# Expert outputs scattered in pair order, x blocks turned by VectorE, gates applied in the final sum

## The chip, the cores and the metric

The kernel runs on one core of a Trainium2 chip. The metric is the device time of one execution in microseconds (us), the median of several runs. The program is written by hand for five engines: TensorE (PE in the profile, with its weight loads as PEld), VectorE (DVE), ScalarE (ACT), GpSimd (POOL) and SyncE (SP). They run their own instruction lists and meet at semaphores. Transfers are carried out by 16 DMA engines. SyncE issues plain transfers on the hardware queue q1. GpSimd issues indirect ones, with a row number per partition, on the software queue q0.

## The reference

The program computes one layer of a hybrid trunk for 128 context tokens and 512 latent tokens of width 1024 (float32): four groups of sequence mixers (gated DeltaNet, HGRN2, mLSTM, Hyena), an output projection, and then a mixture of experts with a final norm. The change concerns the mixture of experts:

```python
scores = sigmoid(t @ router_w)                    # t: 640 tokens x 1024, 64 experts
_, idx = top_k(scores + router_bias, 8)
sel    = take_along_axis(scores, idx)
wts    = sel / sum(sel) * 2.5                     # eight gates of a token
gates  = einsum('tk,tke->te', wts, one_hot(idx, 64))
hid    = silu(t @ w_gate[e]) * (t @ w_up[e])      # 1024 -> 128, every expert
routed = einsum('tef,efd->td', hid * gates[..., None], w_down)
x      = x + gate2 * (routed + shared)            # then the final RMSNorm
```

Only the eight chosen experts of a token have a gate that isn't zero, so a kernel may compute the 640 x 8 = 5120 pairs of token and expert alone.

## The kernel before

Everything up to the router takes until about 880 us and is not touched, but for one thing: between the chunks of the sequence mixers SyncE also fills the last 42 blocks of the DRAM tensor `y_rows` with zeros (L653), and waits for these fills at the end of that part.

**Slots.** The pairs are sorted by expert into blocks of 128 slots. Blocks 0 to 63 belong to the 64 experts, one each; an expert with more than 128 pairs has the rest in spill blocks from 64 on. Their number is known only at run time, in groups of two (`group_count`, at least `LEAST` = 2 groups beyond what is fixed). In these runs there are 70 blocks in all. VectorE makes one-hot matrices of the block and of the slot of every pair (L3070, L3072), ScalarE scales the block matrix by token number less 640 (L3275), and TensorE sums their products in `table(t)`, t = 0 to 4 (L2717). The result, plus 640, is `token_row`: the token of each slot, and 640 in an empty slot. A row number out of bounds is skipped by the indirect DMA. TensorE does these tables between the turning back of the normed x into rows, which SyncE stores to `h2_rows` with a token's 64 gates behind its 1024 values, and the products of the shared expert (L2728).

**A block.** The order on each engine is written out by hand, in a loop of 16 turns of `U` = 4 blocks:
- SyncE loads gate, up and down weights of block b, three transfers of 512 KB, into one of four buffers, once TensorE has done the down product of block b-4 (`load_block`, L2426 to L2428), and stores all 128 rows of an earlier y (`store_block`, L2432).
- GpSimd copies a column of `token_row` (L3400) and gathers 128 rows of x with its gates, 4352 bytes each, into one of four buffers (L3403), once the block four earlier has been turned.
- TensorE turns x by eight 128x128 transposes into PSUM (L2763), does the down product of the block before (L2779, 4 instructions of 512 columns in the trace) and then gate and up of this block (L2771, 32 instructions of 128 columns).
- ScalarE copies the turned x out of PSUM (L3310) and applies silu to the gate product (L3316).
- VectorE picks the gate column (L3089), multiplies silu(gate) by up (L3091), and evicts the down product with the gate as a scale (L3098).

Spill blocks (`spill`) go by pairs in buffers 0 and 1, with the expert read from `block_expert`. The load for such a block waits for the down product of the last block in the same buffer.

**Final sum.** When all stores have landed, GpSimd gathers for each tile of 128 tokens its eight y rows, choice by choice, by `dest_u` (40 indirect transfers of 512 KB, L3432) into `GB` = 14 buffers. TensorE sums choices 4 to 7 with the identity as the weights (L2820), VectorE sums choices 0 to 3 (L3151, L3157), adds the two (L3162), multiplies by gate2 (L3165) and adds to x (L3167). ScalarE sums the squares (L3336) and takes the root (L3339), VectorE scales (L3141), and SyncE stores the tile (L2472).

## Time and profile before

| | |
|---|---|
| runs | 1449.32 us median of 3 (1447.54 to 1451.58) |
| profiled execution | span 1449.8 us, 21596 instructions; no other time is recorded for it |
| busy PE, DVE, ACT, POOL | 1337.0, 685.5, 412.0, 301.5 us |
| TensorE clock | mean granted 0.983 |
| gate and up of block 0 starts | 922.87 us |
| down of the last block (69) starts | 1367.35 us |
| first read of the final sum | 1374.44 us |

The busy share of an engine says how full it is over the whole program, which has stages with different limits. So the shares are read by stage (a table of windows, times from the span's start), and then the chain of waits: the work that ended last, followed back from what each step waited for. The time of a transfer is counted as a share of the 16 DMA engines.

### The profile page before, as it was taken

What the parts mean: (1) busy time and instruction counts of PE and PEld (TensorE: products, weight loads), DVE (VectorE), ACT (ScalarE), POOL (GpSimd) and SP (SyncE); (2) the same over time, 40 slices, a digit from 0 to 9 for tenths busy, and PEclk for the clock granted to TensorE, in tenths of its full rate; (3) what the DMA queues carried; (4) which work ended last, traced back from release to release, by engine and by line L of the source; (5) the groups of instructions that cost most, each with busy time, mean ns of one, the idle gap of its engine ahead of it and who ended that gap; (6) DMA issues with size and microseconds to landing.
All of it is one profiled execution on the core that took longest, in us unless ns stands there. A gap on an engine that the chain in (4) does not pass through costs nothing. (4 is left out here: it accounts for less than half of the span.)

```text
span 1449.8 us, 21596 instructions
## 1 busy us (share of the span) xinstructions
PE 1337.0 (92%) x8160; PEld 996.5 (69%) x8160; DVE 685.5 (47%) x1254; ACT 412.0 (28%) x796; POOL 301.5 (21%) x440
## 2 busy tenths in 40 slices
PE   5999999999899998999799999999999999999664
PEld 1678666777899986555545457688888888887521
DVE  2698738202665663777576226432222222222156
ACT  3212221215556554233131025321222122212111
POOL 0200100102321311454440210211111111111173
PEclk9999999999999999999899999999999999999998
DMA  9656667121433341000120401799999999998696
GB/s 360 209 174 186 201 43 59 58 73 30 182 153 100 127 175 34 8 5 31 37 103 23 175 0 44 281 385 393 384 378 384 378 397 382 398 385 307 212 382 264
DMA packets 111005, 286.36 MB, mean 198 GB/s; under 512 B 28677, under 2 KB 46639, under 8 KB 109528
## 3 DMA queue, kind: packets, MB, share of 16 engines
q1 hardware_dynamic: 95096, 242.15, 48.6%
q0 software_dynamic: 15840, 43.28, 7.8%
q8 instruction: 45, 0.74, 0.2%
q14 instruction: 24, 0.20, 0.0%
HBM read 237.52 MB, written 64.56 MB: 208 GB/s over the span
## 5 line engine op out<-in xcount | busy, mean ns | idle before, releaser
L2771 PEld LDWEIGHTS PS<-arena 128*128 128x128 f32 x2240 | 258.5, 192 | 43.3 <-ACT arena L3310 26.2
L2771 PE MATMUL PS<-arena 128*128 128x128 f32 x2240 | 263.1, 276 | 5.2 <-DMA arena<-in_exp_w_down 3.9
L3098 DVE TENSOR_SCALAR arena<-PS,arena 128x1024 f32<-128x1024 f32 x70 | 89.9, 1284 | 141.6 <-PE PS L2779 141.6
L2779 PE MATMUL PS<-arena 128*128 128x512 f32 x280 | 137.8, 615 | 0.8 <-DVE arena L3091 0.8
L895 PE MATMUL PS<-arena 128*128 128x320 f32 x384 | 109.4, 438 | 1.5 <-DVE arena L1317 1.5
L3316 ACT ACTIVATE arena<-PS 128x128 f32<-128x128 f32 x70 | 19.4, 277 | 312.7 <-issue 176.7
L900 PE MATMUL PS<-arena 128*128 128x320 f32 x384 | 107.3, 432 | 0.0
L3091 DVE TENSOR_TENSOR arena<-arena,PS 128x128 f32<-128x128 f32 x70 | 20.1, 288 | 182.8 <-ACT arena L3316 93.4
L895 PEld LDWEIGHTS PS<-arena 128*128 128x128 f32 x384 | 73.0, 192 | 33.3 <-issue 2.9
L900 PEld LDWEIGHTS PS<-arena 128*128 128x128 f32 x384 | 73.0, 190 | 30.4
L3403 POOL DMA_INDIRECT arena<-h_rows,arena x70 | 72.1, 1030 | 58.4 <-POOL arena L3400 57.6
L3310 ACT ACTIVATE arena<-PS 128x1024 f32<-128x1024 f32 x70 | 71.6, 1023 | 43.6 <-PE PS L2763 43.6
L3400 POOL COPY arena<-arena 128x1 uint32 (+1 forms) x70 | 12.9, 185 | 309.5 <-DVE arena L3089 292.7
L1389 DVE SCALAR_TENSOR_TENSOR arena<-arena 128x1024 f32<-128x1024 f32 x56 | 69.1, 1280 | 15.5 <-DMA arena<-in_w_mod 14.9
L2763 PE MATMUL PS<-cst,arena 128*128 128x128 f32 x560 | 73.0, 273 | 1.6 <-DMA arena<-h_rows,arena 1.6
L2779 PEld LDWEIGHTS PS<-arena 128*128 128x128 f32 x280 | 47.4, 189 | 37.3 <-issue 34.5
L907 PE MATMUL PS<-arena 128*128 128x256 f32 (+1 forms) x320 | 72.2, 387 | 0.0
L907 PEld LDWEIGHTS PS<-arena 128*128 128x128 f32 x320 | 60.6, 190 | 14.7 <-issue 4.3
L2763 PEld LDWEIGHTS PS<-cst,arena 128*128 128x128 f32 x560 | 67.1, 188 | 2.4 <-issue 2.4
L2820 PE MATMUL PS<-arena,cst 128*128 128x512 f32 x80 | 41.4, 641 | 27.9 <-DMA arena<-y_rows,arena 25.4
L1543 DVE TENSOR_TENSOR arena<-PS,cst 128x512 f32<-128x512 f32 x40 | 27.7, 692 | 57.5 <-PE PS L962 57.5
L2593 PE MATMUL PS<-arena 128*128 128x512 f32 x120 | 52.6, 592 | 0.0
(478 smaller groups left out, 2078.0 us busy)
## 6 DMA issues: line engine op xcount, KB each, us to landing
arena<-in_exp_w_gate SPq DMA_DIRECT2D x70, 512.0 KB
arena<-in_exp_w_up SPq DMA_DIRECT2D x70, 512.0 KB
arena<-in_exp_w_down SPq DMA_DIRECT2D x70, 512.0 KB
y_rows<-arena SPq DMA_DIRECT2D x70, 512.0 KB
arena<-in_w_in SPq DMA_DIRECT2D x16, 1024.0 KB, 6.2
arena<-in_w_mod SPq DMA_DIRECT2D x32, 512.0 KB, 3.7
y_rows<-cst SPq DMA_DIRECT2D x2, 5632.0 KB, 18.5
y_rows<-cst SPq DMA_DIRECT2D x2, 5120.0 KB, 18.0
```

The costliest lines, as they stand in the source:

```text
L895: pe.matmul(PS[:, b0, 0:TOK // 2], w[:, k, i * P:(i + 1) * P], hT[:, k, 0:TOK // 2], start=(k == 0), stop=(k == KT - 1))
L900: mm = pe.matmul(PS[:, b1, 0:TOK // 2], w[:, k, i * P:(i + 1) * P], hT[:, k, TOK // 2:TOK], start=(k == 0), stop=(k == KT - 1))
L907: mm = pe.matmul(PS[:, b0, 0:w.shape[2]], src[:, k, i * P:(i + 1) * P], w[:, k, :], start=(k == 0), stop=(k == KT - 1))
L1389: i = dve.scalar_tensor_tensor(out=mod_acc[c], in0=mod_chunk[q % 2], scalar=scond[:, k, c:c + 1], in1=mod_acc[c], op0=ALU.mult, op1=ALU.add)
L2593: pe.matmul(PS[:, OUT_BANK[n], :], yT[:, k, t * P:(t + 1) * P], w_out[k][:, 512 * half:512 * half + 512], start=k == 0, stop=False)
L2763: mm = pe.transpose(PS[:, k // 4, (k % 4) * P:(k % 4 + 1) * P], xg[j][:, k:D:KT], ident)
L2771: mm = pe.matmul(PS[:, bank, 0:P], w[:, k, :], xT[j % 2][:, k, :], start=k == 0, stop=k == KT - 1)
L2779: mm = pe.matmul(PS[:, 4 + 2 * (j % 2) + half, :], hid[j % 2], ed[j][:, 512 * half:512 * half + 512], start=True, stop=True)
L2820: mm = pe.matmul(PS[:, 4 + 2 * (t % 2) + half, :], ident, back[n % GB][:, 512 * half:512 * half + 512], start=k == 4, stop=k == TOPK - 1)
L3098: dve.tensor_scalar(yb[j].rearrange("p (h n) -> p h n", h=2), PS[:, 4 + 2 * (j % 2):6 + 2 * (j % 2), :], gate_col[j % 2], None, ALU.mult). ...
L3310: act.activation(xT[j % 2].rearrange("p (h k) n -> p h (k n)", h=2), PS[:, 0:2, :], ACT.Copy).then_inc(e_xT, 1)
L3403: pool.indirect_dma_start(xg[j], None, T["h2_rows"], bass.IndirectOffsetOnAxis(token_col[j], 0), bounds_check=TOK - 1, oob_is_err=False).t ...
```

## The change

- `h2_rows` holds x only, as 2560 quarter rows of 256 values. The gates are no longer stored with x.
- The table sums the number of the pair (8 x token + choice) in place of the token. GpSimd does the scaling by pair numbers, a matrix now, in place of ScalarE. From the result come `pair_row`, `token_row`, and `quarter_row`: for partition p and quarter g the quarter row of slot 32 g + p mod 32. For this TensorE multiplies four spread identities with the slots' numbers after the shared down products.
- In three of four blocks GpSimd gathers x by four indirect transfers of 128 quarter rows, so that 32x32 turns by VectorE (`turn_x`) give the whole transpose straight in SBUF. Every fourth block (j = 0), and the spill blocks from 66 on, keep the whole-row gather, TensorE's transposes and ScalarE's copy.
- ScalarE takes the down product out of PSUM, unscaled. GpSimd scatters its used rows to `y_rows` in pair order (5120 rows; empty slots are skipped). The zero fills go.
- Blocks 0 to 65 (`FIXED`) are written out; `LEAST` = 3. The order on TensorE is gate and up of b, then the down product of b-1. Gate and up share one PSUM bank, by turns of two.
- In the final sum SyncE reads y by plain loads (pair order makes the rows of one choice a fixed step), and the gates enter here: ScalarE scales choice 0 and makes 20 diagonal matrices for TensorE, VectorE adds choices 1 to 3 with the gate as a scalar. VectorE works the gates out of the router's matrices beside blocks 5 to 9 (`gates_of`).

```diff
-                    q = slice((COLS - NE) * (i - 1) // (PAIRS1 - 1), (COLS - NE) * i // (PAIRS1 - 1))
-                    sp.dma_start(y_spill[:, q], spread(at["strict"][:, 0:D], 1, q.stop - q.start)).then_inc(tail_out, 16)
...
-        LEAST = 2
+        LEAST = 3
+        FIXED = NE + 2
+        FULL = NE // U
...
+        VECTOR = tuple(j > 0 for j in range(U))
...
-                sp.wait_ge(r_g, 1)
-                sp.dma_start(T["h2_rows"].rearrange("(t p) d -> p t d", p=P)[:, :, D:ROW_W], gate[:, :, :]).then_inc(h2_out, 16)
...
-                with sp.Fori(1, NE // U) as i:
-                    for j in range(U):
-                        sp.wait_ge(e_ps, U * i + (j + 1 - U))
-                        load_block(U * i + j, j)
-                        store_block(U * i + (j - U), j)
+                for b in range(U, NE):
+                    sp.wait_ge(e_ps, b - U + 1)
+                    load_block(b, b % U)
...
+                for n in range(PAIRS):
+                    t, k = n // TOPK, CHOICES[n % TOPK]
...
+                    sp.dma_start(back[n % GB], y_pairs[:, t, k]).then_inc(g_in[n % GB], 16)
...
+                pe.wait_ge(m_slots, 2)
+                for g in range(4):
+                    mm = pe.matmul(PS[:, 7, COLS * g:COLS * g + COLS], spread_ident[g].rearrange("p a s -> p (a s)"), slots, start=True, stop=True)
+                mm.then_inc(m_rows, 1)
...
+                for b in range(FIXED):
+                    gate_up(b % U, b // U + 1, by_vector(b), by_tensor(b))
+                    if b + 1 < FIXED and by_vector(b + 1) is None:
+                        transpose_x(b + 1, (b + 1) % U, fetched(b + 1))
+                    if b:
+                        down(b - 1, (b - 1) % U, b <= 2)
...
-                            mm = pe.matmul(PS[:, 4 + 2 * (t % 2) + half, :], ident, back[n % GB][:, 512 * half:512 * half + 512],
+                            mm = pe.matmul(PS[:, 4 + 2 * (t % 2) + half, :], weigh[4 * t + k - 4], back[n % GB][:, 512 * half:512 * half + 512],
...
+                def turn_x(b):
+
+                    j = b % U
+                    dve.wait_ge(e_x[j], fetched(b))
+                    if b >= 2:
+                        dve.wait_ge(e_gu, b - 1)
+                    dve.transpose(xT[j % 2].rearrange("p k (g s) -> p g k s", s=32),
+                                  xg[j].rearrange("p g (i k) -> p g k i", i=32)).then_inc(e_turn, 1)
...
+                for b in range(FIXED):
+                    hidden(b, b % U, b < 2)
+                    if b + 2 < FIXED and by_vector(b + 2) is not None:
+                        turn_x(b + 2)
+                    if b < NT:
+                        own(b)
+                    elif b < 2 * NT:
+                        gates_of(b - NT)
...
-                    dve.tensor_tensor(acc[:, t, :], first, second, ALU.add).then_inc(g_dve, 2)
...
+                        dve.scalar_tensor_tensor(out=acc[:, t, :], in0=row, scalar=gate_of[:, t, k:k + 1], in1=acc[:, t, :],
+                                                 op0=ALU.mult, op1=ALU.add).then_inc(g_dve, 1)
...
+                for b in range(FIXED):
+                    silu(b, b % U, b < 2)
+                    if b + 1 < FIXED and by_tensor(b + 1) is not None:
+                        copy_xT((b + 1) % U, by_tensor(b + 1))
+                    if b:
+                        take_y(b - 1, (b - 1) % U, 16 * ((b - 1) // U) if b > U else None)
...
+                for t in range(NT):
+                    pool.wait_ge(m_beq, t + 1)
+                    pool.tensor_tensor(at_block[t % 2], at_block[t % 2], spread(pair_less[:, t * TOPK:(t + 1) * TOPK], 2, COLS),
+                                       ALU.mult).then_inc(m_bl, 1)
...
+                def gather_quarters(j, rows):
+
+                    for g in range(4):
+                        pool.indirect_dma_start(xg[j][:, g, :], None, T["h2_rows"], bass.IndirectOffsetOnAxis(rows[:, g:g + 1], 0),
+                                                bounds_check=4 * TOK - 1, oob_is_err=False).then_inc(e_x[j], 16)
...
+                def scatter(j, rows):
+
+                    pool.indirect_dma_start(T["y_rows"], bass.IndirectOffsetOnAxis(rows, 0), yb[j], None,
+                                            bounds_check=TOPK * TOK - 1, oob_is_err=False).then_inc(e_out[j], 16)
...
+                def store(b):
+                    if b == 0:
+                        pool.wait_ge(m_tok, 2)
+                    pool.wait_ge(e_y, b + 1)
+                    scatter(b % U, pair_row[:, b:b + 1])
+
+                LAG = 5
+                for b in range(FIXED):
+                    fetch(b)
+                    if b >= LAG:
+                        store(b - LAG)
```

## Rows read from the trace of the kernel before

**Rows 1.** Page, part 1: busy us, share of the span, instructions of each engine.
```profile
PE 1337.0 (92%) x8160; PEld 996.5 (69%) x8160; DVE 685.5 (47%) x1254; ACT 412.0 (28%) x796; POOL 301.5 (21%) x440
```
**Rows 2.** Table of windows: stretch, length, busy us by engine, clock, DMA share, GB/s.
```profile
core 0: us, PE busy (x) PEld busy (x) DVE busy (x) ACT busy (x) POOL busy (x), PEclk, DMA share, GB/s
1000.00:1100.00 100.00, 100.00 (x701) 83.75 (x700) 25.79 (x47) 20.81 (x32) 19.25 (x32) 1.00 1.01 385
1340.00:1368.00 28.00, 24.12 (x166) 19.76 (x167) 5.86 (x12) 4.18 (x7) 2.41 (x4) 1.00 0.78 262
1368.00:1449.80 81.80, 42.68 (x84) 14.30 (x82) 45.26 (x46) 8.04 (x16) 42.34 (x40) 0.89 0.76 295
```
**Rows 3.** Chain of waits in the expert loop: start us, us, what.
```profile
941.84 3.57 PE PS L2771 x32
...
1311.37 0.88 PE PS L2763 x8
1312.25 1.80 PE PS L2779 x4
...
1332.86 3.57 PE PS L2771 x32
```
**Rows 4.** DMA queues from 940 to 1300 us: packets, MB, share of 16 engines.
```profile
q1 hardware_dynamic: 32936, 119.94, 87.3%
q0 software_dynamic: 8209, 19.16, 13.6%
```
**Rows 5.** DMA queues in 1376:1434, 240:260, 225:240 and 923:932, in this order.
```profile
q0 software_dynamic: 5721, 20.87, 93.9%
...
q1 hardware_dynamic: 1098, 1.10, 17.7%
...
q1 hardware_dynamic: 1896, 1.92, 89.0%
...
q0 software_dynamic: 414, 1.09, 31.1%
```
**Rows 6.** Groups by line, 922 to 1338 us: count, busy us, mean ns, idle before.
```profile
L3098 DVE TENSOR_SCALAR arena<-PS,arena 128x1024 f32<-128x1024 f32 x65 | 83.4, 1284 | 130.3 <-PE PS L2779 130.3
L3310 ACT ACTIVATE arena<-PS 128x1024 f32<-128x1024 f32 x67 | 68.6, 1023 | 42.0 <-PE PS L2763 42.0
L3403 POOL DMA_INDIRECT arena<-h_rows,arena x65 | 66.4, 1022 | 54.1 <-POOL arena L3400 53.2 <-issue 0.8
L3091 DVE TENSOR_TENSOR arena<-arena,PS 128x128 f32<-128x128 f32 x66 | 19.0, 288 | 168.2 <-issue 89.5 <-ACT arena L3316 78.8
L3316 ACT ACTIVATE arena<-PS 128x128 f32<-128x128 f32 x66 | 18.3, 277 | 290.0 <-issue 176.7 <-PE PS L2771 113.3
```
**Rows 7.** Timeline ahead of the loop: start us, us, engine, line, instruction, [idle before].
```profile
895.97 2.00 POOL L3389 TENSOR_TENSOR arena<-arena 128x640 f32<-128x640 f32 x1 [33.53 <-ACT arena L3289]
896.86 2.00 PE L2717 MATMUL PS<-arena 128*128 128x106 f32 x16 [1.77 <-ACT arena L3275]
914.70 0.19 POOL L3400 COPY arena<-arena 128x1 uint32<-128x1 uint32 x1 [16.73 <-DMA h_rows<-arena]
```
**Rows 8.** Chain of waits: first gather, a spill block's weights, the last y store.
```profile
915.87 4.44 DMA arena<-h_rows,arena
...
1356.11 6.51 DMA arena<-in_exp_w_down
...
1370.92 2.62 DMA y_rows<-arena
```
**Rows 9.** Timeline of the final sum.
```profile
1375.70 0.95 POOL L3432 DMA_INDIRECT arena<-y_rows,arena  x1 [0.31 <-issue]
...
1393.35 1.77 POOL L3432 DMA_INDIRECT arena<-y_rows,arena  x1 [0.30 <-issue]
...
1430.73 1.22 DVE L3162 TENSOR_TENSOR arena<-arena,PS 128x1024 f32<-128x1024 f32 x1 [5.35 <-remote]
...
1436.64 1.98 PE L2820 MATMUL PS<-arena,cst 128*128 128x512 f32 x4 [0.49 <-DMA arena<-y_rows,arena]
...
1439.76 1.21 DVE L3162 TENSOR_TENSOR arena<-arena,PS 128x1024 f32<-128x1024 f32 x1
```

More of the change, by code:

```diff
@@ L2387, in group_count, with by_vector, by_tensor, fetched @@
             return eng.value_load(block_expert[0:1, P:P + 1], min_val=0, max_val=MOST - LEAST) + LEAST
+        VECTOR = tuple(j > 0 for j in range(U))
+        turns = [sum(VECTOR[c % U] for c in range(b + 1)) for b in range(FIXED)]
+        def by_vector(b):
+            return turns[b] if VECTOR[b % U] else None
+        def by_tensor(b):
+            return None if VECTOR[b % U] else b + 1 - turns[b]
+        def fetched(b):
+            return (64 if VECTOR[b % U] else 16) * (b // U + 1)
+        SPILL_T = FIXED - turns[-1] - 1
+        SPILL_X = [(64 if VECTOR[j] else 16) * (FULL + 1) for j in range(2)]
+        def x_piece(j, k):
+            return xg[j].rearrange("p g c -> p (g c)")[:, k:D:KT]
         with nc.Block() as block:
@@ L2457, in _ @@
                 groups = group_count(sp)
[L2458 to L2462 removed]
+                for b in range(NE, FIXED):
+                    spill_load(b - NE, b % U, b - U + 1)
                 with sp.Fori(1, groups) as i:
@@ L3149, in _ @@
                 for t in range(NT):
[L3150 to L3157 removed]
+                    for k in range(1, 4):
+                        row = choice(t, k)
+                        if k == 1:
+                            dve.wait_ge(g_first, t + 1)
+                        else:
+                            dve.wait_ge(g_dve, 3 * t + k - 1)
+                        dve.scalar_tensor_tensor(out=acc[:, t, :], in0=row, scalar=gate_of[:, t, k:k + 1], in1=acc[:, t, :],
+                                                 op0=ALU.mult, op1=ALU.add).then_inc(g_dve, 1)
+                        if k == 1 and t > 0:
+                            last_mean(t - 1)
                     if t > 0:
@@ new lines, in spill @@
+                def spill(i, before, free):
+                    copy_xT(0, 2 * i + SPILL_T)
+                    take_y(2 * i + (NE - 1), before, free)
+                    silu(2 * i + NE, 0)
+                    copy_xT(1, 2 * i + (SPILL_T + 1))
+                    take_y(2 * i + NE, 0, 16 * i + 16 * FULL)
+                    silu(2 * i + (NE + 1), 1)
+                groups = group_count(act)
+                with act.Fori(1, groups) as i:
+                    spill(i, 1, 16 * i + 16 * (FULL - 1))
@@ new lines, in _, with weigh_out, first_choice @@
+                take_y(2 * groups + (NE - 1), 1, 16 * groups + 16 * (FULL - 1))
+                def weigh_out(t):
+                    for k in range(4, TOPK):
+                        i = act.activation(weigh[4 * t + k - 4], ident, ACT.Copy, scale=gate_of[:, t, k:k + 1])
+                    i.then_inc(g_diag, 1)
+                def first_choice(t):
+                    n = TOPK * t
+                    act.wait_ge(g_in[n % GB], 16 * (n // GB + 1))
+                    act.wait_ge(f_own, NT)
+                    act.activation(acc[:, t, :], back[n % GB], ACT.Copy, scale=gate_of[:, t, 0:1]).then_inc(g_first, 1)
@@ new lines, in fetch @@
+                def fetch(b):
+                    j = b % U
+                    if b >= U:
+                        if VECTOR[j]:
+                            pool.wait_ge(e_turn, by_vector(b - U))
+                        else:
+                            pool.wait_ge(e_tr, by_tensor(b - U))
+                    if b == VECTOR.index(True):
+                        pool.wait_ge(m_quart, 1)
+                    elif b == VECTOR.index(False):
+                        pool.wait_ge(m_tok, 1)
+                    if VECTOR[j]:
+                        gather_quarters(j, quarter_row[:, b, :])
+                    else:
+                        gather_rows(j, token_row[:, b:b + 1])
@@ new lines, in _ @@
+                groups = group_count(pool)
+                for j in range(2):
+                    store(FIXED - LAG + j)
+                    if VECTOR[j]:
+                        fetch_spill(1, j, e_turn, by_vector(NE + j))
+                    else:
+                        fetch_spill(1, j, e_tr, by_tensor(NE + j))
+                for b in range(FIXED - LAG + 2, FIXED):
+                    store(b)
+                with pool.Fori(2, groups) as i:
+                    for j in range(2):
+                        fetch_spill(i, j, e_tr, 2 * i + (SPILL_T - 2 + j))
+                        store_spill(i - 1, j)
@@ L3437 @@
+                for j in range(2):
+                    store_spill(groups - 1, j)
 _IN = ['x_prompt', 'x_sample', 'c', 'state_gdn', 'state_hgrn', 'state_mlstm_c', 'state_mlstm_n',
```

304 lines of the change are left out of this document (138 added, 166 removed).

## The prediction

> **What bounds the kernel now.** I read the page's engine shares first, then the table of windows by stage, then the chain of waits, then the DMA queues of the same stretch. TensorE is busy for 92% of the span [rows 1], and from 1000 to 1100 us for 100.00 of 100 us at the full granted clock, while the DMA share is 1.01 [rows 2]: both are full in the expert loop, and the question is which binds once TensorE has less to do. The chain there is TensorE alone: per block 8 transposes 0.88 us, the down product 1.80, gate and up 3.57 [rows 3], 6.25 together. Gate and up of block 3 starts at 941.84 and of block 65 at 1332.86 [rows 3], so the measured pitch is 391.0/62 = 6.307 us. The transfers of 360 us (57 blocks are issued in it) take 87.3% and 13.6% of 16 engines [rows 4], (0.873 + 0.136) x 6.307 = 6.36 us of all engines per block. So DMA has no room either. Behind the loop lie four spill blocks, where TensorE waits for weights (24.12 of 28 us busy, DMA 0.78), and the final sum, with TensorE at 42.68 of 81.8 us and DMA at 0.76 [rows 2]: a stretch of transfers.
>
> **The change, part by part.**
>
> *Loop, TensorE.* Three of four blocks lose the transposes: 3.57 + 1.80 + 0.25 x 0.88 = 5.59 us per block, against 6.307.
>
> *Loop, DMA.* A MB costs 0.873 x 360/119.94 = 2.62 us on the hardware queue and 0.136 x 360/19.16 = 2.56 on the software queue [rows 4]; 19.16 MB over 57 blocks are 0.336 MB or 77 rows of 4352 B per block. After: weights 1.573 MB x 2.62 = 4.12 us; y rows scattered, 77 x 4 KB = 0.315 MB x 2.62 = 0.83, in place of a full 0.524 MB store (1.37); a whole-row gather 0.315 MB = 0.83. Quarter rows are 1 KB packets: 1.10 MB in 17.7% of 20 us is 3.2 us per MB in one stretch, 1.92 MB in 89.0% of 15 us is 6.95 in another, which follows a heap of tiny packets [rows 5]. I take the first, quieter one: 0.315 x 3.2 = 1.01 (the other: 2.19). Mean gather 0.75 x 1.01 + 0.25 x 0.83 = 0.97. Sum 5.92 us, and divided by the 1.009 that today's account comes to per period (6.36/6.307), 5.87. With the other quarter price it is 6.7. The software queue would need (0.83 + 0.97)/5.9 = 31% of the engines; 31.1% is what it got beside a full weight queue from 923 to 932 us [rows 5], so it is not starved, with nothing to spare.
>
> *Loop, GpSimd.* Today one indirect DMA per block, 1.02 us [rows 6]. After: four quarter gathers and a scatter in three blocks, two instructions in the fourth, 17 per four blocks, 4.25 per block. In an unbroken run one takes 0.95 us and the next follows 0.31 later [rows 9]: 1.26 x 4.25 = 5.4 us; with 1.02 it is 5.7. Below 5.87, but the third engine that is nearly full.
>
> *Loop, VectorE and ScalarE.* The turn of 128x1024 by VectorE isn't in this trace. Bounds: the 0.29 us of the 128x128 product, and four of the 1284 ns passes over 128x1024 [rows 6], 5.1 us; I take 1.3, the same length in one pass, and the eviction of that length, which moves away, pays for it. With the product of 0.29 it fits in 5.9 us up to nearly the upper end. ScalarE takes the y eviction as it did the transposed x, 1023 ns each [rows 6]: with the silu's 0.28, 0.28 + 1.02 + 0.25 x 1.02 = 1.6 us per block. Both are covered; the silu and product of a block now have the next block's whole gate and up product as cover.
>
> DMA is the largest of 5.59, 5.87 and 5.4 to 5.7. I take 5.9: 62 x (5.9 - 6.307) = **-25.2 us**. Unrolling is counted at nothing: the pitch is 0.06 us over the work in it, so the loop's turns can't cost more than that, and 62 x 0.06 = 3.5 us bounds the gain.
>
> *Before the loop.* The scaling of the one-hot blocks moves from ScalarE to GpSimd, behind the shared product, which ends at 895.97 + 2.00 = 897.97 [rows 7]. 128x640 took 2.00 us; 128x848 costs 2.0 to 2.65 by length; I take 2.2. The first table, now at 896.86 [rows 7], starts about 900.2, 3.4 us late, of which about a third goes into TensorE's gaps before the last table: +2.3 at block 0. The fetch loses its column copy, 914.70 to 915.87 [rows 7, 8], which pays for the extra rounding of the token numbers. Quarter numbers come only after the shared down products, the fetch of block 1 takes four instructions (5 us) and 4.44 to land [rows 8], and block 1 starts some 4 us late; blocks 2 and 3 win part back. At block 3, from which I count the loop: **+2.3** (0 to +5). The zero fill of the spill rows and the gate columns of x lie beside other work: nothing.
>
> *Spill.* Down of block 64 now follows gate and up of 65, so the load of block 66 into its buffer is issued 3.57 + 1.80 = 5.4 us after that product starts instead of about 0.2. A load takes some 7.4 us to land (6.51 from the issue of its third part [rows 8]) and paces the spill blocks. Followed on from the start of product 65: 66 lands at 12.8, its down ends at 19.3, 68 lands at 26.7, its down ends at 33, and so 69's at 39.5; today 1369.3 - 1332.9 = 36.5. From that +3 some 0.5 us per load go for the smaller stores beside them: **+2** (0 to +5).
>
> *Into the final sum.* Today the last store lands 2.62 us after issue [rows 8]; an indirect transfer took 4.44 [rows 8], so +1.8; the eviction by ScalarE is 0.26 shorter, and GpSimd's 0.9 us from landing to its first read goes: **+0.7** (-0.5 to +2).
>
> *Final sum.* Today from GpSimd's first read, 1375.70 - 0.31 - 0.95 = 1374.44, to the last data at 1436.64 [rows 9], 62.2 us, with GpSimd's start-up and y stores between the reads. 20.97 MB at 0.939 x 58/20.87 = 2.61 us per MB [rows 5] are 54.7 us; the ramp leaves less of it with 14 loads issued by SyncE at once, and the output stores now queue behind all loads. I take 54: -8.2. VectorE needs 9.0 us a tile now (L3162 of the last two tiles at 1430.73 and 1439.76, in its own time) and 0.2 more with three scaled adds, under 54/5 = 10.8. The gates on ScalarE (20 short ones of 0.28 us) fit under the first loads. The tail is 1449.8 - 1436.64 = 13.2 today, in which VectorE takes up the last sum at 1439.76, 1.1 us after TensorE's end at 1438.62 [rows 9]; 0.8 of it goes. **-9.0** (-13 to 0).
>
> Sum: 2.3 - 25.2 + 2 + 0.7 - 9.0 = -29.2, 1449.8 - 29.2 = 1420.6. The span is 0.5 us over the median of the runs, with nothing else around it: 1420.
>
> **Rivals.** Outside the loop the sum is -4.0 us.
>
> A. TensorE stays the bound at 5.59, 62 x -0.717 = -44.5; 1401. It needs 2.62 us per MB to fall with less traffic. For: TensorE waits for no weights today although its demand fills DMA. Against: a DMA share of 1.01 [rows 2].
>
> B. GpSimd becomes the bound without losing all: at 1.46 us per instruction the pitch is 6.2, loop -6.6; 1439. For: instructions beside VectorE passes with two SBUF operands took 1.77 us [rows 9].
>
> C, the slower side: GpSimd's issue above 1.50 us per instruction (6.37/4.25; there the pitch eats the 4.0 us). In its order of work the scatter of block b-5 stands before the next fetch and four quarters are issued in a row, so each stretched instruction delays x itself. At 1.6 us the pitch is 6.8: 62 x 0.49 - 4.0 = +26.6; 1476. Against: 57 instructions in the loop mean 1.02 [rows 6], with VectorE reading PSUM. The Trainium skill (SBUF — State Buffer, "SBUF: two separate sides") has GpSimd locked out by VectorE instructions in a two-port mode or with two SBUF inputs. By that rule the turn counts only if it runs in such a mode; then up to 1.3 us of each 5.4 is added, which is between B and C. The 1.77 us row agrees with the rule.
>
> D. The reads of the final sum step 8 rows (32 KB) between partitions. If such a step halved their rate, +54 us: 1474. No row has it; today's rows come from as far apart, but in no order. The Trainium skill (DMA: Bandwidth & Descriptors, "Latency and other measured facts") has the rate halve at power-of-two pitches of 4 MiB and hardly fall at 512 KiB, which speaks for a small chance; no run so far shows it.
>
> **Chances.** Forecast 0.48, A 0.15, B 0.19, C 0.13, D 0.05. A measurement tells 0.3%, 4.3 us, from no change. Faster: the first three but for the upper edge of B, 0.77; same 0.06; slower 0.17. The forecast's own range is 1408 to 1434 (pitch 5.7 to 6.1). To hold 8 in 10 the range reaches just past A and, above, past B: 1398 to 1448.
>
> **What would show it.** Right: gate-and-up starts about 5.9 us apart, DMA share near 1.0 with fewer GB/s, TensorE idle 0.3 us per block behind weights; VectorE's turn near 1.3 us; block 1 late by 4 us; last y data 54 us after the first load. Wrong: a pitch of 5.6 with DMA below 1.0 (A); GpSimd without gaps and TensorE waiting for the turn (B, C); the final reads below 300 GB/s (D); a turn above 5 us.

## The result, and the profile after

The changed kernel takes 1463.5 us (median of 6 runs, 1455.2 to 1464.7), the kernel before 1449.9 (6 runs beside it, 1446.7 to 1451.6). The ratio is 1.0085, with a 95% interval of 1.0064 to 1.0107: slower, by 0.9%. Forecast were 1420 us and a chance of 0.17 for slower. The profiled execution took 1459.2 us, its span is 1457.3.

The code ahead of the router did not change, yet its end (the count product, L2707 before and L2737 after) lies at 883.41 us in the profile before and at 879.16 after; in the profiles of this study it lies anywhere from 878.9 to 888.7. So the start of the loop is counted from there.

| step | forecast | measured, us |
|---|---|---|
| ahead of the count product (not changed) | 0 | -4.2 |
| count product to gate and up of block 3: 58.4 -> 68.5 | +2.3 | +10.1 |
| 62 blocks: pitch 6.307 -> 6.370 | -25.2 | +3.9 |
| gate and up of block 65 to the last down product: 36.5 -> 44.6 | +2 | +8.1 |
| last down product to the end: 80.5 -> 70.1 | +0.7 - 9.0 | -10.4 |
| spans | -29.2 | +7.5 |

Page, part 1, answering to [rows 1]:

```profile
PE 1308.3 (90%) x7776; PEld 964.9 (66%) x7776; DVE 701.5 (48%) x1185; ACT 441.2 (30%) x837; POOL 482.3 (33%) x560
```

TensorE lost 28.7 us of work and the kernel took longer. The table of windows, answering to [rows 2]:

```profile
core 0: us, PE busy (x) PEld busy (x) DVE busy (x) ACT busy (x) POOL busy (x), PEclk, DMA share, GB/s
1000.00:1100.00 100.00, 91.91 (x607) 73.88 (x606) 27.91 (x28) 24.92 (x36) 69.65 (x70) 0.98 0.97 350
1343.00:1387.20 44.20, 36.57 (x213) 29.07 (x211) 1.44 (x5) 11.17 (x15) 9.19 (x14) 0.88 0.48 167
1387.20:1457.30 70.10, 41.08 (x80) 14.50 (x80) 44.90 (x45) 20.64 (x42) 0.97 (x1) 0.89 0.85 337
```

In the loop nothing is full now: TensorE idles 8%, and the DMA share fell from 1.01 to 0.97. The chain of waits, answering to [rows 3] and [rows 8] (start us, us, what):

```profile
959.13 3.57 PE PS L2807 x32
962.70 1.73 PE PS L2815 x4
...
965.33 11.54 DMA arena<-in_exp_w_down
...
976.91 3.84 PE PS L2807 x32
980.75 1.73 PE PS L2815 x4
...
983.84 12.64 DMA arena<-in_exp_w_down
...
996.53 5.47 PE PS L2807 x32
...
1348.96 6.05 DMA arena<-in_exp_w_down
1355.01 0.12 issue
1355.13 5.95 PE PS L2807 x32
...
1365.63 6.65 DMA arena<-in_exp_w_down
1372.28 0.12 issue
1372.40 5.46 PE PS L2807 x32
...
1389.19 2.07 DMA y_rows<-arena
```

Before, the chain here was TensorE alone. Now it runs down weights, a few products, down weights again, every 18 to 27 us; after a wait the first product takes 3.84 us, or 5.47 where the granted clock had fallen to 1.2 GHz (half of full speed, from 997.8 to 1001.2 us in the clock's records). The DMA queues from 940 to 1300 us, answering to [rows 4], and the issues of the same stretch with the median us to landing:

```profile
q1 hardware_dynamic: 24164, 88.03, 66.9%
q0 software_dynamic: 18303, 36.30, 28.5%
...
arena<-in_exp_w_gate SPq DMA_DIRECT2D x57, 512.0 KB, 5.5
...
arena<-in_exp_w_down SPq DMA_DIRECT2D x57, 512.0 KB, 12.3
arena<-h_rows,arena POOLq DMA_INDIRECT x186, 9.5
```

A MB now costs (0.669 + 0.285) x 360/124.33 = 2.76 us of all engines, against 2.62, and the engines are full for 0.95. Groups by line, answering to [rows 6] (923 to 1342 us: count, busy us, mean ns, idle before and what ended it):

```profile
L2807 PE MATMUL PS<-arena 128*128 128x128 f32 x2080 | 256.9, 284 | 44.7 <-DMA arena<-in_exp_w_down 36.8 <-DVE arena L3136 6.6 <-ACT arena L3360 1.3
L3469 POOL DMA_INDIRECT arena<-h_rows,arena x196 | 200.3, 1022 | 63.8 <-issue 54.9 <-ACT arena L3354 4.3 <-DVE arena L3127 4.3
L3136 DVE STREAM_TRANSPOSE arena<-arena 128x1024 f32<-128x1024 f32 x49 | 99.3, 2026 | 18.0 <-DMA arena<-h_rows,arena 18.0
L3354 ACT ACTIVATE arena<-PS 128x1024 f32<-128x1024 f32 x63 | 64.5, 1024 | 78.9 <-PE PS L2815 78.9
```

GpSimd, VectorE and ScalarE do what was forecast of them; the turn takes 2.03 us in place of 1.3, in 6 us of room. Ahead of the loop, answering to [rows 7]:

```profile
893.58 4.93 POOL L3460 TENSOR_TENSOR arena<-arena 128x848 f32<-128x848 f32 x2
896.12 3.72 PE L2747 MATMUL PS<-arena 128*128 128x106 f32 x16 [5.28 <-POOL arena L3460]
899.63 1.91 PE L2729 MATMUL PS<-cst,arena 128*128 128x128 f32 x8
...
901.34 2.35 PE L2747 MATMUL PS<-arena 128*128 128x106 f32 x16
...
932.05 2.01 DVE L3136 STREAM_TRANSPOSE arena<-arena 128x1024 f32<-128x1024 f32 x1 [10.59 <-DMA arena<-h_rows,arena]
...
934.21 6.46 PE L2807 MATMUL PS<-arena 128*128 128x128 f32 x32 [6.64 <-DVE arena L3136]
```

The final sum: DMA queue from 1395 to 1440 us, answering to [rows 5].

```profile
q1 hardware_dynamic: 5073, 18.49, 102.7%
```

It moves 411 GB/s where it moved 360 (20.87 MB in 58 us).

### The profile page after: what moved, and what is told of

Read it like the earlier page. It is cut to its first block and busy times, and to the rows that moved or that the text cites. A ratio compares the mean times of both kernels' runs of the same rounds, so it can differ in the third digit from the quotient of the medians.

```text
span 1457.3 us, 20129 instructions
## 1 busy us (share of the span) xinstructions
PE 1308.3 (90%) x7776; PEld 964.9 (66%) x7776; DVE 701.5 (48%) x1185; ACT 441.2 (30%) x837; POOL 482.3 (33%) x560
## 5 line engine op out<-in xcount | busy, mean ns | idle before, releaser
L2807 PEld LDWEIGHTS PS<-arena 128*128 128x128 f32 x2240 | 272.6, 201 | 95.5 <-DMA arena<-in_exp_w_down 66.3
L2807 PE MATMUL PS<-arena 128*128 128x128 f32 x2240 | 279.5, 286 | 51.3 <-DMA arena<-in_exp_w_down 43.4
L3469 POOL DMA_INDIRECT arena<-h_rows,arena x196 | 200.3, 1022 | 63.8 <-issue 54.9
L2815 PE MATMUL PS<-arena 128*128 128x512 f32 x280 | 132.1, 594 | 1.0 <-DVE arena L3143 0.9
L3136 DVE STREAM_TRANSPOSE arena<-arena 128x1024 f32<-128x1024 f32 x49 | 99.3, 2026 | 18.0 <-DMA arena<-h_rows,arena 18.0
L3479 POOL DMA_INDIRECT y_rows<-arena x70 | 72.1, 1030 | 103.4 <-ACT arena L3354 80.2
L892 PEld LDWEIGHTS PS<-arena 128*128 128x128 f32 x384 | 73.0, 192 | 33.3 <-issue 2.9
L897 PEld LDWEIGHTS PS<-arena 128*128 128x128 f32 x384 | 73.0, 190 | 30.4
L1386 DVE SCALAR_TENSOR_TENSOR arena<-arena 128x1024 f32<-128x1024 f32 x56 | 69.0, 1280 | 15.5 <-DMA arena<-in_w_mod 14.9
L2815 PEld LDWEIGHTS PS<-arena 128*128 128x128 f32 x280 | 47.8, 191 | 35.2 <-issue 35.2
L904 PEld LDWEIGHTS PS<-arena 128*128 128x128 f32 x320 | 60.6, 190 | 14.7 <-issue 4.3
L2854 PE MATMUL PS<-arena 128*128 128x512 f32 x80 | 41.1, 642 | 18.9 <-DMA arena<-y_rows 18.9
L1540 DVE TENSOR_TENSOR arena<-PS,cst 128x512 f32<-128x512 f32 x40 | 27.7, 692 | 57.5 <-PE PS L959 57.5
L2236 POOL TENSOR_TENSOR arena<-arena 128x128 f32<-128x128 f32 x70 | 32.1, 495 | 63.4 <-ACT arena L2070 44.7
L2623 PE MATMUL PS<-arena 128*128 128x512 f32 x120 | 52.6, 592 | 0.0
L974 PE MATMUL PS<-arena 128*128 128x128 f32 x400 | 52.1, 283 | 0.0
```

The lines of the kernel that those rows point to most:

```text
L892: pe.matmul(PS[:, b0, 0:TOK // 2], w[:, k, i * P:(i + 1) * P], hT[:, k, 0:TOK // 2], start=(k == 0), stop=(k == KT - 1))
L897: mm = pe.matmul(PS[:, b1, 0:TOK // 2], w[:, k, i * P:(i + 1) * P], hT[:, k, TOK // 2:TOK], start=(k == 0), stop=(k == KT - 1))
L904: mm = pe.matmul(PS[:, b0, 0:w.shape[2]], src[:, k, i * P:(i + 1) * P], w[:, k, :], start=(k == 0), stop=(k == KT - 1))
L1386: i = dve.scalar_tensor_tensor(out=mod_acc[c], in0=mod_chunk[q % 2], scalar=scond[:, k, c:c + 1], in1=mod_acc[c], op0=ALU.mult, op1=ALU.add)
L2623: pe.matmul(PS[:, OUT_BANK[n], :], yT[:, k, t * P:(t + 1) * P], w_out[k][:, 512 * half:512 * half + 512], start=k == 0, stop=False)
L2807: mm = pe.matmul(PS[:, j % 2, col:col + P], w[:, k, :], xT[j % 2][:, k, :], start=k == 0, stop=k == KT - 1)
```

## The experiments

First the theories. **L (lead):** the load of block b is issued after the down product of b-4, which now stands behind gate and up of b-3, so it has 5.4 us less; gate and up wait for all three weights. **T:** the DMA engines can't carry more. **Q:** quarter rows are dear. **E**, formed after the first four runs: the 16 engines are loaded unevenly, since only about 77 of a block's 128 slots are used and these lie on the first partitions; a load has landed when the last engine has. The trace doesn't name the engine of a packet, so E is tested by what it foretells.

All kernels beside each other. "Start" is from the count product to block 3, "pitch" over 62 blocks, "spill" to the last down product, all from the matmul records; DMA share, GB/s and TensorE's idle time ahead of gate and up are of 960 to 1320 us. These come from one profiled execution per kernel. e3_early and e10_first4 have the same loop from block 4 on and show 6.170 and 6.394, so a difference of pitch under 0.2 us between kernels that wait for weights is not read as an effect. Medians in us; the kernel before ran beside each at 1449.6 to 1452.6.

| kernel | time | ratio (95%) | start | pitch | spill | DMA, GB/s | idle |
|---|---|---|---|---|---|---|---|
| before | 1449.9 | | 58.3 | 6.307 | 36.6 | 1.01, 385 | 0 |
| after | 1463.5 | 1.0085 (1.0064-1.0107) | 68.4 | 6.370 | 44.8 | 0.96, 348 | 34.9 |
| e1_order | 1463.7 | 1.0087 (1.0057-1.0117) | 72.1 | 6.521 | 35.2 | 0.96, 339 | 12.2 |
| e2_split | 1452.7 | 1.0008 (0.9986-1.0030) | 67.7 | 6.419 | 39.0 | 0.96, 345 | 38.3 |
| e3_early | 1444.5 | 0.9964 (0.9945-0.9982) | 68.3 | 6.170 | 34.5 | 0.98, 358 | 27.7 |
| e4_rows | 1482.9 | 1.0210 (1.0181-1.0239) | 64.3 | 6.763 | 45.4 | 0.92, 325 | 23.1 |
| e5_spread | 1538.3 | 1.0549 (1.0463-1.0635) | 70.8 | 7.462 | 42.1 | 0.83, 290 | 49.0 |
| e6_spread_early | 1528.7 | 1.0542 (1.0495-1.0588) | 70.4 | 7.576 | 34.4 | 0.83, 292 | 37.8 |
| e7_spread_rows | 1469.7 | 1.0140 (1.0116-1.0164) | 63.6 | 6.591 | 43.4 | 0.93, 336 | 16.6 |
| e8_nogather | 1417.7 | 0.9772 (0.9746-0.9798) | 68.2 | 5.648 | 45.5 | 0.94, 330 | 9.8 |
| e9_flip_early | 1404.2 | 0.9684 (0.9657-0.9712) | 68.5 | 5.616 | 35.5 | 1.00, 382 | 4.4 |
| e10_first4 | 1447.9 | 0.9980 (0.9963-0.9997) | 63.4 | 6.394 | 34.7 | 0.96, 346 | 38.8 |
| e11_flip | 1419.7 | 0.9794 (0.9762-0.9825) | 69.0 | 5.670 | 43.5 | 1.00, 380 | 10.9 |
| e12_best | 1396.6 | 0.9635 (0.9606-0.9663) | 62.5 | 5.542 | 34.8 | 0.98, 378 | 0.9 |
| e13_flip_rows | 1443.8 | 0.9939 (0.9919-0.9959) | 64.4 | 6.167 | 42.0 | 0.99, 359 | 0 |
| e14_before_flip | 1454.1 | 1.0021 (1.0001-1.0042) | 67.0 | 6.281 | 36.3 | 1.02, 388 | 0 |
| e15_quads_rows | 1440.1 | 0.9923 (0.9900-0.9946) | 63.2 | 6.167 | 43.5 | 0.99, 359 | 0 |
| e16_quads_best | 1502.1 | 1.0363 (1.0324-1.0402) | 59.0 | 7.320 | 34.9 | 0.83, 296 | 53.3 |

**e1_order**

```diff
                 for b in range(FIXED):
+                    if b:
+                        down(b - 1, (b - 1) % U, b <= 2)
                     gate_up(b % U, b // U + 1, by_vector(b), by_tensor(b))
...
-                    if b:
-                        down(b - 1, (b - 1) % U, b <= 2)
```

and on ScalarE the y eviction of b-1 ahead of the silu of b.

> Blocks 0 to 65 with the order of before: the down product of b-1 ahead of gate and up of b (and the y eviction ahead of the silu). Theory L (lead): the weights of block b are asked for only once down of b-4 is done, which now stands behind gate and up of b-3, so they have 5.4 us less to land, and landing takes 12.4 us. Undone, TensorE's waits for down weights (66 us in the changed kernel) fall below 15 us, and what binds is the silu and the product between gate and up of b-1 and its down: 3.57 + 1.80 + 0.22 + about 0.9 = 6.3 to 6.5 us per block instead of 6.37, the last loads' stretch gains 3 to 5 us. Total 1455 to 1465. Rival T (throughput): the DMA engines carry 2.2 MB per block at 2.75 us per MB and can't do better than 6.1 whatever the order; waits for weights stay at 40 us or more.

TensorE's waits for weights fell from 34.9 to 12.2 us and the spill blocks won 9.6 us, as lead says. (The 66 us of the expectation are the idle time of the weight loads, PEld; TensorE's products waited 36.8 of the same stretch.) But TensorE now idles 28.9 us ahead of the down product, for VectorE's product behind the silu, and the start is 3.7 us later; the total didn't move.

**e2_split**

```diff
-                    sp.dma_start(ed[j], ...).then_inc(e_w[j], 16)
+                    sp.dma_start(ed[j], ...).then_inc(e_d[j], 16)
...
-                    pe.wait_ge(e_w[j], 48 * loaded)
+                    pe.wait_ge(e_w[j], 32 * loaded)
...
+                    pe.wait_ge(e_d[j], 16 * loaded)     # in down
```

> The down weights get a semaphore of their own: gate and up wait for two transfers (landing in 6.9 us), down for the third (12.4 us). Theory L: gate and up of b no longer wait for a transfer that is needed 5.4 us later; pitch from 6.37 to 6.0 to 6.1, where DMA at 2.75 us per MB binds; -17 to -23 us in the loop, about 1443. Rival T in its pure form (the engines give no more bytes than now): the wait moves from gate and up to down, pitch stays at 6.3 or more, 1458 or more.

The total lies between the two forecasts. A miss for L in the loop: the pitch of the profile isn't below that of the changed kernel (the 10.8 us of the medians, less 5.7 in the spill blocks, leave it some 4 to 5 us), and the wait went to the up weights, which now landed after 13.2 us (median) in place of 7.0. That the second of three transfers issued together takes 13 us is what brought up theory E. The spill blocks won 5.7 us.

**e3_early**: e2_split, and

```diff
-                    sp.wait_ge(e_ps, b - U + 1)
-                    load_block(b, b % U)
+                    sp.wait_ge(e_gu, b - U + 1)
+                    load_in(b, b % U)       # gate and up
+                    sp.wait_ge(e_ps, b - U + 1)
+                    load_down(b, b % U)
```

and the same for the spill blocks.

> As the split, and gate and up weights of block b are asked for as soon as gate and up of b-4 are done, one down product earlier than their buffer's third part. Theory L: another 1.8 us of lead for two of three transfers; the DMA share of the loop goes to 1.0, pitch 5.9 to 6.1, and the spill blocks gain 3 us or more; 1436 to 1443. Rival T: as the split, within 4 us of it.

Lead is worth something: 19 us by the medians, 10 of it in the spill blocks; L had forecast more. Its profiled execution (1437.2 us) was the quickest of its runs, so its pitch flatters it. The up weights landed after 18.2 us, still too late. TensorE's group of gate and up from 945 to 1340 us:

```profile
L2820 PE MATMUL PS<-arena 128*128 128x128 f32 x2044 | 245.9, 279 | 27.7 <-DMA arena<-in_exp_w_up 27.7
```

**e4_rows**

```diff
-        VECTOR = tuple(j > 0 for j in range(U))
+        VECTOR = tuple(False for j in range(U))
```

> All blocks gather whole rows and are turned by TensorE (no quarter rows, no turn by VectorE); everything else as changed. Rival Q (quarter rows cost the DMA engines more than their bytes, and so stretch the landings): 2.62 us per MB again, down weights land in 9 us or less, TensorE waits for them under 15 us, pitch at TensorE's work 6.25 to 6.3, total about 1455. Theory L: landing stays above 11 us, the lead is three pitches less 5.4; waits for weights fall only because the pitch is longer, pitch 6.4 to 6.5, total 1465 to 1470.

Q is wrong: without quarter rows the DMA share fell to 0.92 and the pitch rose by 0.39 us, above L's forecast too. A quarter-row gather puts its rows on other partitions than its slots, a whole-row gather does not: this agrees with E, but doesn't show it yet.

**e5_spread**

```diff
-  at_slot[t % 2][:, :, :] <- spread(iota, 1, TOPK) is_equal lo
+  at_slot[t % 2].rearrange("p c (e k) -> p c e k", k=8)
+      <- spread(iota.rearrange("p (k e) -> p e k", e=16), 1, TOPK) is_equal lo
```

> The changed kernel with one line changed: the pair of rank 16 k + e in its block goes to slot 8 e + k, so that the about 77 used slots of a block lie on all partitions in place of the first 77. The bytes, the counts of transfers and the order of work stay. Theory E (uneven DMA engines): a transfer gives each of the 16 engines 8 neighbouring partitions, so the scattered y rows and the whole-row gathers lie on 10 engines; these carry 24 + 8 + 5.6 packets of 159 ns = 6.0 us and about 0.2 of small elements per block, while the mean is 5.5, and a load has landed only when the last engine has. Spread: every engine 33.6 packets, 5.5 us; down weights land below 10 us, the waits for weights fall below 20 us, pitch 5.7 to 6.0, total 1425 to 1440. Theory L (lead) alone: the share of an engine does not matter, pitch 6.35 to 6.39, total within 4 us of the changed kernel. If an engine instead gets every 16th partition, this makes it uneven: pitch above 6.6.

None of the three as described. The pitch of 7.46 is above the 6.6 of the last one, but the profile shows gaps of a kind that no kernel before it had (timeline):

```profile
1110.01 5.40 PE L2807 MATMUL PS<-arena 128*128 128x128 f32 x32 [2.87 <-DMA arena<-in_exp_w_down]
...
1118.52 1.00 POOL L3469 DMA_INDIRECT arena<-h_rows,arena  x1 [0.30 <-issue]
...
1121.43 0.28 ACT L3348 ACTIVATE arena<-PS 128x128 f32<-128x128 f32 x1 [13.21 <-DMA arena<-in_state_mlstm_m]
```

The product is shown as done at 1115.4, and the silu that waits for it starts at 1121.43. Such gaps between the last finished gate and up product and the silu (over 0.5 us, 945 to 1340 us) sum to 78.8 us here, 89.7 in e6_spread_early, and to 0 in the changed kernel: about what the two lost (77 us by the spans against the changed kernel, 90 against e3_early).

**e6_spread_early**: e3_early and e5_spread together.

> The spread slots together with the split semaphore and the earlier gate and up loads. Theories E and L together: engines at 5.5 us and lead enough, TensorE's own 5.59 us is left as the bound; pitch 5.6 to 5.8, spill stretch 35 us, total 1405 to 1420. Theory L alone: as the early loads without the spread, 6.17, total 1440 to 1447.

The same gaps. It tells nothing of lead.

**e7_spread_rows**: e4_rows and e5_spread together.

> Whole-row gathers and TensorE's transposes in all blocks, with the spread slots. Theory E: that kernel's hot engines carried 24 + 8 + 8 packets (6.4 us and more, pitch 6.76 measured); spread, they carry 33.6 and the pitch goes to TensorE's work, 6.25 to 6.35, total 1448 to 1457. If quarter rows by themselves had helped the DMA, the pitch stays above 6.5.

```profile
L2807 PE MATMUL PS<-arena 128*128 128x128 f32 x1742 | 206.8, 277 | 16.6 <-DMA arena<-in_exp_w_down 16.4
```

A miss for E as it then stood: no gaps and 13 us less than e4_rows, but the pitch stays 0.3 us above TensorE's work of 6.25, in the range of the rival (above 6.5). In the DMA records from 1000 to 1300 us, 14 packets or fewer are in flight for 24% of the time (e4_rows 31%, the changed kernel 19%, the kernel before 4%), and hardly ever fewer than 8, as if half the engines went idle together. So I took this spread for no even one, and the 8 neighbouring partitions per engine of the expectation for wrong; e9, e13 and e15 are the tests of that.

**e8_nogather**

```diff
-                        gather_quarters(j, quarter_row[:, b, :])
+                        gather_quarters(j, quarter_row[:, b, :], 4 * TOK - 1 if b < 2 * U else 0)
```

and the same for whole rows; the last argument is the highest row number that isn't skipped.

> The changed kernel; from block 8 to 65 the gathers of x move (almost) no rows: every row number above 0 is skipped, so x of an earlier block is used again. Issues, waits and order stay; left out are 0.3 MB per block. Theory T (what the DMA engines can carry binds): 1.9 MB at 2.75 us per MB are 5.2 us, below TensorE's 5.59; landing of the down weights falls below 8 us, waits for weights below 10 us, pitch 5.6 to 5.75, total 1415 to 1425. Rival I (not the traffic but the chain of issue, turn and eviction holds the loop): pitch stays above 6.1.

T's numbers, 5.65 and 1417.7: issue, turn and eviction don't hold the loop, the traffic does. TensorE is busy for 350.2 of the 360 us at a DMA share of 0.94, so this run doesn't tell whether it was the sum of the traffic or its evenness.

**e9_flip_early**: e3_early, and after rank `lo` and block `hi` of a pair are known:

```diff
+  dest = hi - 2 * round(hi / 2 - 0.25)      # 1 in odd blocks; eight short VectorE steps in all
+  lo   = lo + dest * (127 - 2 * lo)
```

> The kernel with the earlier gate and up loads, and in every second block the slots are used from the top (slot 127 - rank). A block's used slots stay neighbours, so its quarter gathers are as dense as before; but over two blocks the scattered and gathered rows lie on all partitions in place of the first 77. Theory E (uneven engines): pitch from 6.17 to 5.8 to 6.0, DMA share up to 1.0, total 1428 to 1438, with about 1 us more ahead of the loop for eight small VectorE steps. Without it: pitch 6.15 to 6.2, total 1444 to 1448.

E, and more than it forecast: 40 us less than e3_early. The same bytes go at 382 GB/s in place of 358, the up weights land after 11.0 us in place of 18.2, and TensorE is the bound (353.9 of 360 us busy), with the DMA engines as full. From 960 to 1300 us, all within the loop, 131.45 MB take 100.9% of 340 us: 2.61 us per MB, the price of the kernel before.

**e10_first4**: e3_early, with blocks 0 to 3 by whole rows (`vec = [b >= U and VECTOR[b % U] ...]`).

> The kernel with the earlier gate and up loads, and blocks 0 to 3 gather whole rows and are turned by TensorE. Start of block 3, counted from the router's count product, is 68.3 us there and 58.3 in the kernel before; in the kernel with whole rows everywhere it is 64.3. If the quarter rows' late index and four issues make that difference: 64.0 to 64.8, total 1439 to 1442. If the difference is the later table alone: 68, total 1444.

The start is 4.9 us sooner: the quarter rows' late index and four issues cost that much in blocks 1 to 3. The total missed its forecast (1447.9 against 1439 to 1442): the loop, whose code is that of e3_early, shows 6.39.

**e11_flip**: the changed kernel with the alternating slots alone.

> The changed kernel with the alternating slots alone; one semaphore for all three weights and the late loads stay. If the unevenness was the whole cause in the loop: down weights land below 10 us, under the lead of 3 x 5.6 - 5.4 = 11.4 us, pitch 5.6 to 5.7, waits below 10 us; the spill blocks keep their 44 to 45 us; total 1411 to 1418. If the short lead costs by itself also on even engines: pitch 5.8 to 6.1, total 1423 to 1440.

```profile
960.00:1320.00 360.00, 349.13 (x2370) 283.37 (x2369) 121.46 (x126) 98.25 (x142) 262.47 (x261) 1.00 1.00 380
...
arena<-in_exp_w_down SPq DMA_DIRECT2D x62, 512.0 KB, 9.4
```

(The windows' row and the landing of the down weights.) This one edit is worth 43.8 us by the medians, and (6.370 - 5.670) x 62 = 43.4 in the loop. From 1000 to 1300 us 14 packets or fewer are in flight for 2% of the time, against 19% in the changed kernel. The spill blocks keep their 43.5. The total is 1.7 us above its range's upper end, the waits 0.9.

**e12_best**: e9_flip_early, e10_first4, and on GpSimd

```diff
+                pool.wait_ge(m_idx, 16)
+                for t in range(NT):
+                    if t == 2:                # shared product behind two scalings
+                        ... shid ...
```

> Alternating slots, split semaphore and earlier loads, blocks 0 to 3 by whole rows, and GpSimd scales the block matrices of tiles 0 and 1 ahead of the shared product. Against the alternating kernel with early loads (1404.2): block 3 starts 5 us sooner by the whole rows and 1 to 2.5 us sooner by the scaling; pitch stays at TensorE's 5.6 us. Total 1396 to 1400.

```profile
960.00:1320.00 360.00, 357.38 (x2452) 293.43 (x2451) 113.82 (x122) 102.75 (x148) 257.79 (x261) 1.00 0.98 378
```

Faster than both kernels: 0.9635 of the one before. The start is 6.0 us sooner than e9's, 5 of it as in e10 and 1 by the scaling.

**e13_flip_rows**: e4_rows with alternating slots.

> Whole-row gathers and TensorE's transposes in all blocks, with alternating slots. If the engines' uneven load is the cause and alternating evens it for every kind of row: pitch from 6.76 to TensorE's work, 6.25 to 6.35, waits for weights below 8 us in 360, total 1450 to 1458. If alternating helps only through the quarter rows: pitch 6.5 or more, total above 1465.

Better than both: TensorE waits for nothing and the pitch is its own work, from 6.76 to 6.17 us. E holds for whole rows too. Beside e11_flip it also prices quarter rows and turns by VectorE, with engines even: 24 us gained, 31 in the loop less 5 at the start.

**e14_before_flip**: the kernel before with alternating slots.

> The kernel before with alternating slots. It stores all 128 y rows of a block and TensorE (6.25 us per block) waits for nothing, so if the change brought the uneven load with its scatter, nothing is gained: pitch 6.29 to 6.31, total 1448 to 1453, about 1 us more ahead of the loop. If the kernel before was held by it too: 1440 or less.

Nothing gained in the loop (6.281), in which TensorE waits for nothing with either order of slots: the kernel before, with its store of all 128 rows, did not pay for the uneven gathers. The start was 8.7 us later, not 1: the ten steps took VectorE 3.5 us ahead of the first one-hot matrix, and one of them stood for 1.43 us beside GpSimd's product. TensorE then idled 5.1 us, the granted clock was 1.2 GHz from 899.3 to 906.1 us, and the last table starts 5.8 us later by the count product; the first gate and up product ran at 1.2 GHz again (5.94 us in place of 3.81).

**e15_quads_rows**: e4_rows, and the one-hot slots compare with

```diff
+  rank of partition p = 64 * (p // 32 % 2) + 16 * (p % 4) + 8 * (p // 64) + p // 4 % 8
```

> Whole rows and TensorE's transposes in all blocks; rank r of a block goes to the slot whose partition has the bits (r3, r6, r2, r1, r0, r5, r4), so 16 neighbouring ranks lie on 16 groups of four partitions, those of both halves alike. Assumption Q: an engine serves two groups of four partitions, 32 apart, of one half (0 to 63 or 64 to 127). By it the first 77 slots put 8 rows on each of 8 engines and 13 on the rest; slot 8 e + k puts 8 rows on every second engine and 1 or 2 on the others, so it was no evener, which fits 6.59 beside 6.76 us; this one puts 4 or 5 on each. Expected: as with alternating slots, pitch 6.16 to 6.2 (TensorE's work), no waits for weights, 1440 to 1448. If Q is wrong: waits of 15 us or more in 360 and a pitch above 6.4. The Trainium skill (DMA: Bandwidth & Descriptors, 'The descriptor swizzle') is where assumption Q is from.

```profile
L2808 PE MATMUL PS<-arena 128*128 128x128 f32 x1861 | 217.3, 275 | 0.0
```

Where slot 8 e + k left 16.6 us of waits (e7), this one leaves none. So "anything but the first slots" is not the rule, and the assumption on which partitions share an engine passes: it told beforehand that this order is even, and it accounts for the first 77 slots (8 rows on each of 8 engines) and for 8 e + k, which was hardly better (8 rows on every second engine). The Trainium skill has that assignment (DMA: Bandwidth & Descriptors, "The descriptor swizzle": in a transfer to 128 partitions engines 0 to 7 write partitions 0 to 63 and 8 to 15 the others, four neighbouring partitions and the four 32 further each), and the floor of 8 packets in flight agrees. No run tells an engine that is full from a full way into these partitions of SBUF; for where to put the rows it makes no difference.

**e16_quads_best**: e12_best with e15's slots.

> As the best kernel so far (split semaphore, early loads, whole rows in blocks 0 to 3, scaling first), with this assignment in place of the alternating one. By assumption Q every block is even by itself: whole rows and y rows 4 or 5 per engine, pitch 5.5 to 5.6, total 1393 to 1400. Rival: what stopped the quarter-row kernels with slot 8 e + k (gaps of 9 us between a gate and up product and its silu, pitch 7.5) comes from quarter gathers in which all four are partly filled, not from uneven engines; then these gaps return and the total is above 1450.

The rival. The start is the best of all (59.0), and then the gaps return: 70.1 us of them. But its wording was too wide: here two of a block's four quarter gathers are full. What e5, e6 and e16 have in common, and no kernel without gaps has in such numbers, are packets of 1036 bytes, by their size one used quarter row and three skipped ones (832, 792 and 792 of them from 960 to 1320 us), and 905 to 956 with two and three used rows; the changed kernel has 28 of the first and 113 of the others. That these bring the gaps is not shown, and how stays open: a product that is shown as done 9 to 12 us ahead of its silu can't be read from this trace.

## Why the prediction was wrong

**The step that failed** is "DMA is the largest of 5.59, 5.87 and 5.4 to 5.7. I take 5.9" and the sentence under it that the software queue "is not starved, with nothing to spare". It summed the transfers over 16 engines and took the sum to be the limit. The sum was even a little too high: with even engines it measures 2.18 MB x 2.61 = 5.7 us per block (e9_flip_early, 960 to 1300 us), because quarter rows are no 1 KB packets at 3.2 us per MB but 4096-byte ones of 159 ns. The limit that the runs show is the most loaded engines: the pitch was 6.370, 0.5 over the 5.87, with down weights landing after 12.3 us and TensorE waiting 34.9 of 360 us for them. The change took the full y store, which loads all engines alike, and put in its place a scatter of 77 rows from the first partitions, by the assignment that e15 bears out mostly on eight engines, the same that the whole-row gathers use. Evened out (e11_flip), the loop runs at 5.67, 0.2 below the forecast. The rows on record had nothing against it: DMA share 1.01, and gathers known only in bulk [rows 2, 4].

**The lead** was seen for the spill blocks ("Down of block 64 now follows gate and up of 65") and not for the 62 blocks ahead, where every load is issued later by the same 5.4 us. Its worth, by the medians: 19 us with uneven engines (after to e3_early, 10 of it in the spill blocks), 15.5 with even ones (e11 to e9). Of these the profiles show 8.0 in the spill blocks and 3.3 in the loop; 3.6 lie ahead of the count product, which the edit doesn't touch.

**Before the loop**, +2.3 against +10.1. The first table starts 3.5 us later by the count product, as forecast. That a third would go into gaps was wrong: the last table ends 5.3 us later. TensorE had idled 5.28 us for the first one, the granted clock was 1.2 GHz from 895.4 to 902.2 us, and the first table took 3.72 us in place of 2.00, the turning group behind it 1.91 in place of 1.04; no later table waited for GpSimd. Block 1 starts another 4.1 us late, as forecast, but "blocks 2 and 3 win part back" didn't show: behind its wait of 6.64 us the product of block 1 took 6.46 us at 1.2 GHz, and block 3 is 0.8 later still. Whole rows in blocks 1 to 3 take 4.9 us of this away (e10).

**Spill**, +2 against +8.1: the cause was right (e1, e3 and e9 take it away), and the load of block 66 landed 7.0 us and that of 68 8.1 us after issue, against the 7.4 assumed. What the sum lacked is the clock: behind the two waits the products of blocks 66 and 68 ran wholly or in part at 1.2 GHz and took 5.95 and 5.46 us in place of 3.57, 4.3 of the missing 6.1 us. The gain from smaller stores didn't show.

**Final sum**, -9.0 and +0.7 against -10.4: right in the main. The last data came 53.9 us after the first load was issued, against 54. Between the last down product and the first load it is -1.0 in place of +0.7, since the last scatter landed in 2.07 us, not 4.44. Steps of 32 KB between the partitions read at 411 GB/s, so rival D is out.

**Rivals.** A's pitch is what the loop has once the engines are even (5.54 to 5.67), but the changed kernel isn't there. B and C are out: GpSimd's instructions mean 1022 ns beside VectorE's turns, as in the kernel before, which has no turns. So the lock-out of rival C is not seen with these turns. The slower outcome came by a mechanism that was not on my list.

**That the totals nearly agree** in e11_flip (1419.7 against 1420) is chance: the loop is 14 us better than forecast, start and spill 13 us worse, the end 2 better.

## What to carry to other kernels

A DMA share near 1 (0.96 here) says that the engines are busy on average, not that the work on them is even; where a transfer skips rows, count the rows per engine, and place the used ones so that each engine gets its part. When TensorE's order is changed, follow for every block how long before its use a load is issued, not only at the end of the loop. Give transfers that are needed at different times semaphores of their own, but do not expect a gain before the landing itself is right.

## What the hardware showed that was not expected

- The place of 77 used rows among 128 partitions, with the same bytes and counts, moves a loop by 11% (6.370 to 5.670 us) and the DMA rate from 348 to 380 GB/s.
- The second of three 512 KB loads issued within 1.3 us took 7.0 us to land in the changed kernel and 13.2 in e2, which issues them alike. Asked for earlier it took 18.2 us with uneven engines (e3) and 11.0 with even ones (e9).
- VectorE turns 128x1024 float32 by 32x32 squares in 2.03 us. An indirect transfer of 128 rows costs GpSimd 1.02 us and 0.30 until the next, also when it skips nearly all rows (1.02 in e8).
- Quarter rows of four neighbouring partitions appear as one 4096-byte packet of 159 ns, as dear as a whole row.
- After idle stretches of 5.28, 6.64 and 4.65 us TensorE's next work ran at 1.2 GHz, and the gate and up product behind such a wait took 6.46 and 5.95 us in place of 3.57; behind most waits in the loop it took 3.84. So a wait can cost more than its own length.
- Quarter gathers in which used and skipped rows stand side by side in some 1700 packets of 360 us come with gaps of up to 11.8 us in which products, silu and new loads stand still while the DMA share is 0.83 (e5, e6, e16). The cause is open.
